# Causal convolution of a two-block model: 31 taps per channel, or a block transform with constant cosine and sine matrices

## The reference, cut to what matters

```python
def conformer_conv(hn, w_pw1, b_pw1, w_dw, b_dw, ln_g, ln_b, w_pw2, b_pw2):
    u = hn @ w_pw1 + b_pw1                      # 1024 -> 2048
    a, g = jnp.split(u, 2, axis=-1)
    u = a * jax.nn.sigmoid(g)                   # 256 tokens x 1024 channels
    kern = w_dw[:, None, :].astype(u.dtype)     # 31 taps for every channel
    u = lax.conv_general_dilated(u, kern, window_strides=(1,),
        padding=((CONV_WIDTH - 1, 0),), dimension_numbers=("NWC", "WIO", "NWC"),
        feature_group_count=D_MODEL) + b_dw     # causal, each channel alone
    u = layernorm(u, ln_g, ln_b)
    u = jax.nn.silu(u)
    return u @ w_pw2 + b_pw2

hn = rmsnorm(h, mix_norm[0]);  h = h + conformer_conv(hn, ...)
hn = rmsnorm(h, ffn_norm[0]);  h = h + square(relu(hn @ ffn_w1[0])) @ ffn_w2[0]
```

## Time and profile before

| | us |
|---|---|
| median of 3 runs | 2294.61 (2293.03 to 2296.98) |
| profiled execution | 2298.04, its span 2296.2 |
| experts and their planning | about 534 to 1603 of the span |
| convolution module, projection on | about 1613 to 1661 |
| taps after the projection | 1661 to 1717 |
| norm, silu, second product | 1717 to 1761 |

### The profile page before, as it was taken

How to read it: one execution, slowest core, us unless ns; L and a number is a source line. 1 busy time by engine, 2 the same in 40 slices (tenths; PEclk the granted TensorE clock), 3 DMA queues, 4 the chain that set the end, 5 groups by cost and what they waited for, 6 DMA issues and landing times.

```text
span 2296.2 us, 28306 instructions
## 1 busy us (share of the span) xinstructions
PE 2183.3 (95%) x10482; PEld 1769.3 (77%) x10482; DVE 1739.7 (76%) x1671; ACT 1457.3 (63%) x1592; POOL 124.0 (5%) x129
## 2 busy tenths in 40 slices
PE   8999999989999999999888888888999999999998
PEld 7787887877878888886666666666787888888887
DVE  5676545768879888899898989898796566676656
ACT  5644444466767777778777777776675446664445
POOL 0001000005900000000000000000001000000000
PEclk9999999999999999999999999999999999999999
DMA  8307645728899999999999999999413555424652
GB/s 310 108 1 239 202 164 193 251 80 328 344 367 395 395 395 375 394 371 395 386 394 378 394 383 394 381 395 376 161 63 105 200 209 195 172 84 147 220 178 80
DMA packets 275545, 608.58 MB, mean 265 GB/s; under 512 B 10661, under 2 KB 47777, under 8 KB 274784
## 3 DMA queue, kind: packets, MB, share of 16 engines
q1 hardware_dynamic: 271616, 593.80, 70.9%
q0 software_dynamic: 3776, 13.13, 1.6%
q10 hardware_dynamic: 32, 0.02, 0.0%
HBM read 592.74 MB, written 14.16 MB: 264 GB/s over the span
## 4 chain that ended last, share of the span: by engine, by line
PE 63%; DMA 15%; DVE 10%; ACT 4%; POOL 4%; issue 3%; SPq 0%; DVEq 0%; ACTq 0%; POOLq 0%
DMA raw<-in_moe_w_up 11%; PE up L2592 6%; PE up L2598 6%; PE up L2593 6%; PE acc L3431 5%; DVE wl L2069 5%; DMA raw<-in_moe_w_gate 4%; PE up L3065 4%; PE up L3069 4%; PE up L3072 3%; PE acc L3436 3%; PE tp L3398 2%; PE up L3398 2%; DVE arena L2257 2%; ACT wh L1251 2%
## 5 line engine op out<-in xcount | busy, mean ns | idle before, releaser
L2069 DVE TENSOR_TENSOR wl<-raw,wh 128x2048 fp32r<-128x2048 f32 x378 | 859.6, 2289 | 111.9 <-ACT wh L1251 110.5
L1251 ACT ACTIVATE wh<-raw 128x2048 fp32r<-128x2048 f32 x378 | 724.6, 1921 | 201.6 <-DMA raw<-in_moe_w_up 46.9
L1740 DVE TENSOR_TENSOR wl<-raw,wh 128x2048 fp32r<-128x2048 f32 x168 | 384.5, 2291 | 272.5 <-ACT wh L988 271.3
L988 ACT ACTIVATE wh<-raw 128x2048 fp32r<-128x2048 f32 x168 | 322.0, 1918 | 280.0 <-PE up L2598 104.8
L2592 PE MATMUL up<-wh,xT 128*128 128x512 f32 x608 | 241.5, 398 | 2.1 <-ACT half L1029 0.8
L2593 PE MATMUL up<-wh,xT 128*128 128x512 f32 x608 | 237.0, 390 | 0.0
L3084 PE MATMUL up<-wl,xT 128*128 128x512 f32 x560 | 158.9, 405 | 28.1 <-DVE wl L2069 26.5
L2598 PE MATMUL up<-wl,xT 128*128 128x512 f32 x608 | 162.8, 390 | 0.1
L3081 PE MATMUL up<-wh,xT 128*128 128x512 f32 x560 | 155.7, 400 | 3.0 <-ACT wh L1251 2.7
L3084 PEld LDWEIGHTS up<-wl,xT 128*128 128x128 f32 x560 | 99.8, 188 | 74.8 <-DVE wl L2069 56.5
L2592 PEld LDWEIGHTS up<-wh,xT 128*128 128x128 f32 x608 | 115.0, 189 | 27.9 <-issue 4.0
(11 more groups left out here) (508 smaller groups left out, 3493.3 us busy)
## 6 DMA issues: line engine op xcount, KB each, us to landing
raw<-in_moe_w_gate SPq DMA_DIRECT2D x126, 1024.0 KB, 13.6
raw<-in_moe_w_up SPq DMA_DIRECT2D x126, 1024.0 KB, 14.0
raw<-in_moe_w_down SPq DMA_DIRECT2D x126, 1024.0 KB, 12.9
raw<-in_ffn_w SPq DMA_DIRECT2D x64, 1024.0 KB, 5.4
raw<-in_hg_w_in SPq DMA_DIRECT2D x15, 1024.0 KB, 12.2
raw<-in_da_w_in SPq DMA_DIRECT2D x12, 1024.0 KB, 5.5
raw<-in_ffn_w_gate SPq DMA_DIRECT2D x22, 512.0 KB, 6.0
raw<-in_ffn_w_up SPq DMA_DIRECT2D x22, 512.0 KB, 7.3
```

The costliest lines, as they stand in the source:

```text
L988: f(wh[:, q % SPLITS, :], raw_half(q), ACT.Copy).then_inc(s_hi, 1)
L1251: f(wh[:, x % SPLITS, :], raw[:, x % RAW, :], ACT.Copy).then_inc(moe["hi"], 1)
L1740: V.tensor_tensor(wl[:, q % SPLITS, :], raw_half(q), wh[:, q % SPLITS, :].bitcast(F32), ALU.subtract).then_inc(s_lo, 1)
L2069: V.tensor_tensor(wl[:, x % SPLITS, :], raw[:, x % RAW, :], wh[:, x % SPLITS, :].bitcast(F32), ALU.subtract).then_inc(moe["lo"], 1)
```

## The change

The convolution of a block of 128 tokens with 31 taps is 158 rows long, so a cyclic transform of TERMS = 160 points holds it; its real half has FREQ = 81 frequencies. Constant matrices lie as a table of 128 x 964 behind `hg_tables`: cosines and sines for 128 tokens (`wave_in`), for the 31 taps (`wave_taps`), the way back for 158 rows (`wave_out`), and a row that picks the bias (`bias_row`).

- The table (128 x 964), the taps (31 x 1024) and the conv's bias row are loaded by SP in the first expert's sixth round, behind `fetched`. POOL's load of the taps, their transposes on PE and the copy to `wdw` on ACT are gone.
- When the projection begins, PE multiplies the taps by `wave_taps` (4 f32 products of 81 x 512) in the place of five `keep_busy` products, and ACT copies the result to `tap_waves` (`keep_taps`, 6 copies of 81 x 512).
- In the middle of each chunk PE takes a step's `stage`, token rows as they are, to 81 frequencies (`to_waves`, 2 f32 products of 81 x 256) instead of turning it.
- DVE multiplies by the taps' spectrum (`spectrum`: two products over 81 x 512, one difference and one sum over 81 x 256).
- PE brings the sums back to token rows in `acc` (`from_waves`): the bias for both blocks when b = 0 (2 products), 2 products for the own block, and 2 more for the 30 rows that run over from block 0 to block 1.
- The DVE taps, ACT's diagonals, PE's taps, the turns back, `residual` and its 4 products are gone. The rows' statistics read `acc`. h + bias is made by two DVE additions of 128 x 1024 ahead of the last additions. One weight half is split ahead of step 7.

```diff
@@ SP, first expert, sixth round
                     ld(fetched[0:rows_after.shape[0], :], rows_after, moe["fetched"])
+                    if before is None:
+                        sp.wait_ge(s_ppe, 4)
+                        ld(fourier, t["hg_tables"][:, H_END:H_END + F_END], cv_tables)
+                        ld(tap_rows[0:CONV, :], t["conv_w_dw_2"][0], cv_tables)
+                        ld(tap_rows[CONV:CONV + 1, :], t["conv_b_dw_2"][0:1, :], cv_tables)
@@ ACT
+        def keep_taps(i, n):
+            act.wait_ge(cv_taps, 2 * i + n + 1)
+            for x in ((0, 2) if i == 0 else (1,)):
+                f(tap_waves[:, x, n * W:(n + 1) * W], acc[0:FREQ, 2 * i + n, :], ACT.Copy).then_inc(cv_spectrum, 1)
...
                 f(half[:, b, HALF:W], half[:, b, HALF:W], ACT.Sigmoid).then_inc(s_act, 1)
+                if c == 0:
+                    for n in range(2):
+                        keep_taps(b, n)
+                if (c, b) == (3, 0):
+                    split()
@@ DVE
+        def spectrum(s):
+            tt, cols_ = t_cv[s], slice(s // NB * HALF, (s // NB + 1) * HALF)
+            dve.wait_ge(s_T, tt + 1)
+            if s == 0:
+                dve.wait_ge(cv_spectrum, 6)
+            else:
+                dve.wait_ge(cv_sum, s)
...
+            V.tensor_tensor(wave_products[:, 0], waves, tap_waves[:, 0:2, cols_], ALU.mult).then_inc(cv_product, 1)
+            V.tensor_tensor(wave_products[:, 1], waves, tap_waves[:, 1:3, cols_], ALU.mult).then_inc(s_Te, 1)
...
+            V.tensor_tensor(wave_sums[:, s % 2, 0], wave_products[:, 0, 0], wave_products[:, 0, 1], ALU.subtract)
+            dve.wait_ge(s_Te, tt + 1)
+            V.tensor_tensor(wave_sums[:, s % 2, 1], wave_products[:, 1, 0], wave_products[:, 1, 1], ALU.add).then_inc(cv_sum, 1)
...
+            if s >= 2:
+                spectrum(s - 2)
+            if s == 6:
+                split()
...
-        dve.wait_ge(s_Te, t_cv[5] + 1)
-        for j in range(CONV):
-            if j == CONV - EARLY:
-                split()
-            tap(j, CV_DVE[2:] if j < 2 * EARLY else CV_DVE)
+        dve.wait_ge(cv_out, 3)
+        V.bn_stats(bnd[:, 0, :], acc[:, 0, :])
+        for s in (6, 7):
+            spectrum(s)
...
+            link(V.tensor_tensor(h[:, b, :], h[:, b, :], rows[:, 0:D], ALU.add))
@@ PE
-                    keep_busy(acc[:, 3, :], 5)
+                    pe.wait_ge(cv_tables, 3 * 16)
+                    for i in range(2):
+                        for n in range(2):
+                            mm(acc[0:FREQ, 2 * i + n, :], wave_taps[:, i, :], tap_rows[:, n * W:(n + 1) * W], start=True,
+                               stop=True).then_inc(cv_taps, 1)
+        def to_waves(g, tt, nk):
+            n = g - g_cv
+            pe.wait_ge(s_st, g + 1)
+            turn_bank(tt)
+            for i in range(2):
+                ins = mm(tp[0:FREQ, tt % 2, i * HALF:(i + 1) * HALF], wave_in[:, i, :], stage[:, g % 2, 0:HALF], start=True, stop=True)
+            ins.then_inc(s_T, 1)
+            if n >= 2:
+                from_waves(n - 2)
+        def from_waves(n):
...
+            for at_b in range(NB if b == 0 else 0):
+                mm(acc[:, 2 * at_b + c // 2, at], bias_row, tap_rows[:, c * HALF:(c + 1) * HALF], start=True, stop=False)
+            pe.wait_ge(cv_sum, n + 1)
+            for i in range(2):
+                ins = mm(acc[:, 2 * b + c // 2, at], wave_out[:, i, 0:P], wave_sums[:, n % 2, i], start=False, stop=i == 1)
+            if b == 0:
+                for i in range(2):
+                    ins = mm(acc[:, 2 + c // 2, at], wave_out[:, i, P:2 * P], wave_sums[:, n % 2, i], start=False, stop=False)
+            ins.then_inc(cv_out, 1)
```

More of the change, by code:

```diff
@@ L79 @@
 NS = NL - JOINED + 1
+TERMS = 160
+FREQ = TERMS // 2 + 1
+F_IN, F_TAPS = 0, 2 * FREQ
+F_OUT = F_TAPS + 2 * FREQ
+F_BIAS = F_OUT + 4 * P
+F_END = F_BIAS + P
 H_MASK, H_LEV, H_TRI, H_END = 0, NL * P, 16 * P, 17 * P
@@ L116, in constant_table, with fourier_table, waves @@
     c[:, C_ONES:C_ONES + P] = 1.0
-    return c, hg
+    return c, np.concatenate([hg, fourier_table()], 1)
+def fourier_table():
+    c = np.zeros((P, F_END), np.float32)
+    turn = 2 * np.pi / TERMS
+    f = np.arange(FREQ)
+    weight = np.where(f % (TERMS // 2) == 0, 1.0, 2.0)[:, None] / TERMS
+    def waves(at):
+        angle = turn * (at[:, None] * f[None, :] % TERMS)
+        return np.cos(angle), -np.sin(angle)
+    c[:, F_IN:F_TAPS] = np.concatenate(waves(np.arange(P)), 1)
+    c[0:CONV, F_TAPS:F_OUT] = np.concatenate(waves(CONV - 1 - np.arange(CONV)), 1)
+    rows = P + CONV - 1
+    for i, part in enumerate(waves(np.arange(rows))):
+        c[0:FREQ, F_OUT + 2 * P * i:F_OUT + 2 * P * i + rows] = weight * part.T
+    c[CONV, F_BIAS:F_END] = 1.0
+    return c
 def head_rows():
@@ L1422, in _ @@
         split(1)
-        def conv_sum(i):
-            k = CV_PE[i]
-            act.wait_ge(cv_tap, CONV * (i + 1))
-            f(cT[:, k, :], acc[:, i, 0:SEQ], ACT.Identity, bias=rowcols[:, 0, k:k + 1]).then_inc(cv_sum, 1)
-        def diagonals(xs):
-            for x in xs:
-                if x >= DIAGS:
-                    act.wait_ge(cv_tap, x - DIAGS + 1)
-                if x % CONV == DIAGS and x > CONV:
-                    conv_sum(x // CONV - 1)
-                f(diag[:, x % DIAGS, :], ident, ACT.Copy, scale=wdw[:, CV_PE[x // CONV], x % CONV:x % CONV + 1]).then_inc(cv_diag, 1)
+        def keep_taps(i, n):
+            act.wait_ge(cv_taps, 2 * i + n + 1)
+            for x in ((0, 2) if i == 0 else (1,)):
+                f(tap_waves[:, x, n * W:(n + 1) * W], acc[0:FREQ, 2 * i + n, :], ACT.Copy).then_inc(cv_spectrum, 1)
         for c in range(4):
@@ L1440, in _ @@
                 split()
-                for b in range(NB):
-                    step_copy(t_cv[NB * (c - 1) + b], uT[:, :, PADC:], c - 1, b, 2)
-            if c >= 2:
-                diagonals(range(EARLY_DIAGS * (c - 2), EARLY_DIAGS * (c - 1)))
             for b in range(NB):
@@ L2283, in _ @@
                     split()
[L2284 to L2287 removed]
         dve.sem_inc(s_rows_free, 1)
[L2289 to L2294 removed]
+        dve.wait_ge(cv_out, 3)
+        V.bn_stats(bnd[:, 0, :], acc[:, 0, :])
+        for s in (6, 7):
+            spectrum(s)
         for b in range(NB):
             for q in range(2):
[L2297 to L2298 removed]
+                dve.wait_ge(cv_out, 7 + b if q == 1 else 3 + b)
+                if (b, q) != (0, 0):
+                    ins = V.bn_stats(bnd[:, q, :], acc[:, 2 * b + q, :])
             link(ins)
@@ L2311, in _ @@
         for b in range(NB):
+            link(V.tensor_tensor(h[:, b, :], h[:, b, :], rows[:, 0:D], ALU.add))
+        for b in range(NB):
             dve.wait_ge(s_acc, A_PW2 + b + 1)
@@ L2314, in _ @@
                 at = slice(q * W, (q + 1) * W)
-                V.tensor_tensor(h[:, b, at], acc[:, 2 * b + q, :], rows[:, at], ALU.add).then_inc(s_h, 1)
+                V.tensor_tensor(h[:, b, at], acc[:, 2 * b + q, :], h[:, b, at], ALU.add).then_inc(s_h, 1)
             if b == 0:
@@ L2701, in behind @@
                     if s >= 0 and ts[s] is not None:
-                        turn_step(g0 + s, ts[s], nk)
+                        (turn_step if step is None else step)(g0 + s, ts[s], nk)
             for c in range(chunks):
@@ L3293, in _ @@
+        project(g_cv, t_cv, 4, T_cv, 2, enter_cv, bank_read=lambda g: pe.wait_ge(cv_n, g - 1 - g_cv), step=to_waves)
+        for n in (6, 7):
+            from_waves(n)
         for x, (b, q) in enumerate(COLUMNS):
@@ L3295, in _ @@
             turn_place(T_cn, ctm, x, COLUMNS)
-        out_product(T_cn, lambda: turn_ready(after[0]["T_f"], H_F[0], BLOCK[0]), COLUMNS)
+        out_product(T_cn, lambda: turn_ready(after[0]["T_f"], H_F[0], BLOCK[0]), COLUMNS, start=True)
         for i, d in enumerate(after):
```

108 lines of the change are left out of this document (29 added, 79 removed).

## The result

The changed kernel took 2279.72 us (median of four runs, 2277.15 to 2282.4), the kernel before in the same series 2293.94. The ratio is 0.993, with a 95% interval of 0.9915 to 0.9944: faster by 14 us, where 25 were predicted. 2279.72 lies above the range of 2262 to 2277.

The account below looks back on a forecast made before the run. VectorE's taps were taken to bound the convolution module; +13.6 projection, -44.8 tail, +1.3 h additions, +1.8 SP loads and +3.0 clock sum to -25.1 us, from 2294.6 to 2269.5, range 2262 to 2277.

Parts of the forecast that it names:

- What bounds the kernel: Convolution module: VectorE's taps lead the chain of waits, almost two thirds of the stretch, with PE's taps the next limit.
- Projection +13.6: Projection on PE: tap spectra +2.55, `to_waves` +4.14, `from_waves` +6.94 us, all on the path, with VectorE hidden.
- Tail -44.8, with the clock -41.8: Projection's end to `out_product`: 20.7 us instead of 65.5, so -44.8; a clock fall adds +3.0.
- The walk at full clock, 20.7 us: Projection's end to `out_product`: sum of split, low part, step 7, three spectra, statistics, aggregates and the last 5.7 us.
- The clock term: Tail: one fall to 1.2 GHz stretches last `from_waves`, turns and first `out_product` products; +3.0 us, bounds 0 and 5.
- The sentence that the last `from_waves` hides behind the statistics: Tail: PE's last `from_waves`, 0.87 us, hides behind three statistics and two aggregates, 2.15 us.
- h additions +1.3: Behind `out_product`'s start: two VectorE bias additions, about 1.28 us each, against a 1.22 pause; +1.3 us, bounds 0 and 2.5.
- SP in the first expert +1.8, bounds 0 and 3.1: First expert: three loads ahead of the weights, 1.6 us of bytes overlapping 1.0 to 1.5 of issues, delay PE.
- the slower one: Rival, projection: products filling 32 or 81 rows bring half clock, 54 us more, 2323; chance 0.03 with anything else eating the gain.
- The clock holds: Rival, tail: short f32 products break the pauses, no clock fall, 2266.5 us; shares the forecast's 0.72.
- VectorE's spectra: Tail: 2.06 us each; a rival had 4, VectorE setting the pace, 2276 to 2282; 0.20 together with early fall.
- 0.20 on 2273 to 2282: Chance given to the two rivals of an early clock fall in the tail or slow VectorE spectra.

## Why the prediction was wrong, step by step

- *What bounds the kernel*: right. VectorE's taps were the limit; without them the stretch from the projection's end shrank by 40 us.
- *Projection +13.6*: right in mechanism and size. At full clock it is +13.1 to +13.5 (63.5 to 63.8 against 50.3); a product on 81 or 32 rows cost what one on 128 cost at the same clock (four on 32 rows 3.66 us, on 128 rows 3.60), and VectorE stayed hidden. The profiled execution had +15.1, since the clock fell behind the 32-row products.
- *Tail -44.8, with the clock -41.8*: measured -40.1. The walk at full clock, 20.7 us, was right (20.6, with the pause filled and the later fall taken off). The clock term was mis-sized, 3.8 to 4.8 instead of 3.0, within its bounds, and misplaced. It was put at the last products, the turns and `out_product`; the fall there came, but cost 0.4. The rest, 3.4 to 4.4, fell on all six groups of wave products behind the pause ahead of step 7, and these, not VectorE, then set the statistics' start. The sentence that the last `from_waves` hides behind the statistics failed at half clock.
- *h additions +1.3*: measured +1.2.
- *SP in the first expert +1.8, bounds 0 and 3.1*: **this step failed.** It was sized by bytes and issues. It measured +9.1 in the profiled executions and 10 us in the medians, both ways (taken out of the changed kernel, put into the one before). The tap rows alone make 7 of it, by their 31 rows in one load on SyncE's queue. The upper bound, issues plus bytes, had left out that a load may be spread unevenly. The shape was in the diff; the trace of before had this load only from GpSimd's queue, where it landed in 3.4 us, and a row of it on SyncE's queue was not there to be read.
- *Of the rivals*, the slower one named something that exists: the products on 32 rows and 81 columns, six times over, ran at 1.2 GHz for over 30 us. In the projection they were followed by a lower clock for 6 to 8 us in two of eight profiles and for none in six; a projection at half clock did not come. (Its 54 us of PE work is not worked out; by the prediction's own figures, 48 us from 1613 to 1661 and 13.6 more, it would be 62.) "The clock holds" was wrong. VectorE's spectra ran at 1.9 to 2.1 us, not 4.
- *The start of the first expert's weights* was taken as fixed. The issue of the fetched rows came 2.2 us earlier in the profiled execution of after, a lead that was there when the planning began; it hides a part of the loads' cost in the spans.

The chances put 0.20 on 2273 to 2282, for reasons of TensorE's clock and VectorE. The time fell there, mainly by a cause that was not among them.

## What to carry to other kernels

Before a load goes ahead of one that an engine waits for, look at its count of rows as well as its bytes, and whether the queue stands still a few lines earlier: here 124 KB in 31 rows on SyncE's queue cost 7 us, in 16 and 15 rows nearly nothing, and ahead of an idle wait nothing. The 3.4 us that the same load took on its old queue did not tell this. An instruction that waits, put in front of the last step of a stage, cost twice here: its own wait and 3.4 to 4.4 us of the clock that TensorE lost meanwhile. Where a price hangs on a stage whose start moves between executions, measure from the event that starts it.

## What of the hardware was not expected

- A load of 124 KB in 31 rows kept 1 MB of weights issued behind it back by 7 us, and SyncE's own issue of two loads took 9.15 us instead of 1.32, while the DMA engines were busy at a mean share of 0.95 and moved 5.0 MB up to ScalarE's first use. The same 31 rows from GpSimd's queue had landed in 3.4 us in the kernel before.
- Products on 32 rows and 81 columns held the granted clock at 0.50 for over 30 us without a pause of TensorE; on 128 and 128 it stayed at 1.00.
- GpSimd's planning began between 538.3 and 542.2 us in the 16 profiles of all kernels and ended, by the issue of the fetched rows, between 626.5 and 633.9. By GpSimd's rows, which are rough, one and the same small instruction takes 0.33 us in one execution and 2.37 in another (L944 at 631.38 in the changed kernel, at 629.00 in the one with the split moved).
